# A prologue by feature tiles: the modulation of each tile is made while the dense products run, and x is asked for in halves

## The chip, the cores and the metric

One core of a Trainium2 chip runs the whole program. The metric is device time in microseconds of one execution; smaller is better. The core's engines run beside each other and wait for one another by semaphores: TensorE (PE, with its weight loads PEld), VectorE (DVE), ScalarE (ACT), GpSimd (POOL) and SyncE (SP), which here asks for nearly all transfers.

## The reference, cut to what matters

The reference is a two-block model over 1024 tokens of 1024 features, with 256 context tokens beside them. The change concerns only what comes before the first block's mixer:

```python
def rms_norm(x, g):
    return x * lax.rsqrt(jnp.mean(x * x, axis=-1, keepdims=True) + RMS_EPS) * g

def modulate(h, shift, scale):
    return h * (1 + scale) + shift

mod = jax.nn.silu(c) @ ada_w[l] + ada_b[l]
sh1, sc1, g1, sh2, sc2, g2 = ...          # split in six
csh1, csc1, ... = silu(c_ctx) @ ada_w[l] + ada_b[l]
hc = modulate(rms_norm(ctx, norm1_g[l]), csh1, csc1)
hx = modulate(rms_norm(x, norm1_g[l]), sh1, sc1)
# then both go through w_in, in products of 128 columns at a time
```

So before the first dense product the kernel needs the root of each token's mean square, and for each feature a gain `(1 + scale) * norm1_g` and a shift. Scale and shift for x and context are the first 2048 columns of a product of two vectors of 1024 (silu of c and of c_ctx) with an 8 MB matrix.

## The kernel before

Features lie on partitions: x is held as 8 feature tiles (kt or k, 0 to 7) of 128 partitions by tokens. Tokens are in three groups g: 0 is the context (256 tokens), 1 and 2 are the halves of x (512 each). Each dense product is made with three matmuls per feature tile (high by high, high by low, low by high part), since h and the weights are both split in a high part in a reduced type (h_hi, `fp32r`) and a low part that holds the rest (h_lo). "w", "g", "v", "k", "r" are names of 128-column tiles of w_in; a "chunk" is one such tile for one group of tokens, in one of four PSUM banks.

All of it is in `projections`. Each engine has its own program, in an order written out by hand, and no engine passes an instruction that waits.

SP (lines 251 to 275) asks for: the vectors, matrix tile 0, the context, two sets of constants, matrix tile 1, half 1 of x, matrix tile 2, half 2 of x, matrix tile 3, the weight "w", matrix tiles 4 to 7, c_in, then weights "g", "v", "k". The matrix tiles are cut by input feature: tile i is rows 128i to 128i + 127 with all 2048 output columns, and there are three places for them. All weights pass through one buffer `raw_in`; `load_w` waits until the weight before was split.

TensorE: `modulations` (334 to 351) multiplies the 8 matrix tiles as they land; the sum over tiles is whole only after the last. Between them it makes the sums of squares of the groups (`sums`, L331). Then four small matmuls (L350), the picks, turn the rows of the result into columns, one value per partition. Then `first_dense` (353 to 369) makes "w" of the context and "w" and "g" of both halves together, feature tile by feature tile as the parts of h come. Then `dense("v", 0, 0)` (L105) and all that follows.

ACT: squares and roots of the groups (L615, L619, L621; each root takes two table loads), split of "w" (L530, high part), copy of the modulation rows (L633), then all h_hi (L608), 8 of the context and 16 of x. After them it applies silu to c_row, splits "v" and reads the first chunks.

DVE: folds the squares (L910, L912), multiplies x by the root in three passes (L917), makes the gains (L922, L926), then per feature tile the full value (L936) and h_lo (L941). POOL makes the low parts of the weights (L744).

Rows of the profile name memory by the program's names: b_tmp, b_xin, b_ada_in, b_wpool, b_ps (PSUM). The lines that matter for the picks are these:

```python
for j in range(4):
    mm = nc.tensor.matmul(ps[3][:, 8 * j:8 * (j + 1)], mod_rows[:, P * j:P * (j + 1)], row_picks, start=True, stop=True)
```

## Time and profile before

| | |
|---|---|
| time, median of 3 runs | 2264.8 us (2264.53 to 2266.89) |
| profiled execution, its span | 2265.7 us |
| TensorE busy | 2050.2 us, 90% |
| VectorE busy | 1500.4 us, 66% |
| ScalarE busy | 892.1 us, 39% |
| GpSimd busy | 773.6 us, 34% |
| mean granted TensorE clock | 0.957 |

The profile is of one execution; its span runs from the first to the last instruction and lies 0.9 us above the median of the timed runs. Busy shares are means over stages with different limits: the stretch that the change touches is the first 82 us, 3.6% of the span, in which TensorE is idle for long stretches. A clock of 1.00 is 2.4 GHz, 0.50 is 1.2 GHz.

### The profile page before, as it was taken

Reading aid. Unit: us, or ns where it says so; the run is one execution under the profiler, and the core shown is the slowest. Engines: PE = TensorE matmul, PEld = TensorE weight load, DVE = VectorE, ACT = ScalarE, POOL = GpSimd, SP = SyncE. Lnnn points to the kernel's source line nnn. Section 1 sums busy time; section 2 is a strip of 40 time slices with the busy share of each in tenths; the row PEclk is TensorE's granted clock in tenths of the full one; section 3 lists DMA queues with packets and bytes.
Section 4 is the critical chain, followed back from the end, with each engine's and each line's share of the span. In section 5 each row is a group of like instructions: output and inputs, shape, how many; then the busy total and the mean of one; then the engine's idle time right before and its main releaser. Section 6 shows DMA issues by size and latency. Waiting matters only on the chain. (4 is left out here: it accounts for less than half of the span.)

```text
span 2265.7 us, 37012 instructions
## 1 busy us (share of the span) xinstructions
PE 2050.2 (90%) x15072; PEld 1594.0 (70%) x15072; DVE 1500.4 (66%) x2052; ACT 892.1 (39%) x1445; POOL 773.6 (34%) x460
## 2 busy tenths in 40 slices
PE   4989999837878898999999979999899999999898
PEld 1767677636767676788877768887677776776566
DVE  5777767679774548788988870454746676546644
ACT  5453443414434637333333331443434354333320
POOL 1144433300030145877777724533321111111111
PEclk7999999958899999999999999999999999999899
DMA  7535444597655422122221274523211111102512
GB/s 308 182 122 174 151 141 130 154 264 197 167 177 143 159 75 75 56 84 84 84 76 73 84 272 139 177 73 122 85 56 56 66 38 47 66 19 84 195 47 84
DMA packets 181335, 271.16 MB, mean 120 GB/s; under 512 B 74280, under 2 KB 122024, under 8 KB 176816
## 3 DMA queue, kind: packets, MB, share of 16 engines
q1 hardware_dynamic: 164816, 250.57, 33.9%
q10 hardware_dynamic: 16352, 18.22, 2.7%
q8 instruction: 121, 1.98, 0.4%
q14 instruction: 46, 0.38, 0.1%
HBM read 200.53 MB, written 68.23 MB: 119 GB/s over the span
## 5 line engine op out<-in xcount | busy, mean ns | idle before, releaser
L105 PE MATMUL b_ps<-h_hi,b_wpool 128*128 128x512 f32 (+1 forms) x896 | 277.4, 387 | 10.8 <-POOL b_wpool L744 10.8
L2995 PE MATMUL g_ps<-g_h_hi,w 128*128 128x512 f32 x784 | 260.0, 403 | 6.0 <-ACT g_q L3192 5.9
L3313 POOL TENSOR_TENSOR w<-raw_down,w 128x1024 fp32r<-128x1024 f32 x38 | 94.5, 2488 | 464.6 <-ACT w L3168 464.6
L2262 DVE SCALAR_TENSOR_TENSOR e_vars<-grid,vec,e_vars 128x1024 f32<-128x1024 f32 x168 | 216.0, 1285 | 7.4 <-ACT e_vars L2009 4.2
L105 PEld LDWEIGHTS b_ps<-h_hi,b_wpool 128*128 128x128 f32 x896 | 167.8, 192 | 56.3 <-POOL b_wpool L744 14.4
L2995 PEld LDWEIGHTS g_ps<-g_h_hi,w 128*128 128x128 f32 x784 | 149.3, 190 | 40.8 <-ACT g_q L3192 6.9
L105 PE MATMUL b_ps<-h_lo,b_wpool 128*128 128x512 f32 (+1 forms) x448 | 170.6, 381 | 0.0
L2995 PE MATMUL g_ps<-g_h_lo,w 128*128 128x512 f32 x392 | 156.1, 398 | 0.0
L2674 POOL TENSOR_TENSOR g_down_lo<-raw_down,g_down_hi 128x1408 fp32r<-128x1408 f32 x26 | 86.7, 3339 | 142.5 <-ACT g_down_hi L2574 142.5
L2513 PE MATMUL g_pb<-g_z_hi,g_down_hi 128*128 128x512 f32 x286 | 114.8, 401 | 14.7 <-DVE g_down_lo L2751 9.8
L744 POOL TENSOR_TENSOR b_wpool<-raw_in,b_wpool 128x1024 fp32r<-128x1024 f32 x26 | 67.9, 2611 | 173.2 <-ACT b_wpool L530 173.2
L2513 PE MATMUL g_pb<-g_z_hi,g_down_lo 128*128 128x512 f32 x286 | 113.1, 396 | 0.0
L2513 PE MATMUL g_pb<-g_z_lo,g_down_hi 128*128 128x512 f32 x286 | 112.7, 394 | 0.0
L1989 ACT ACTIVATE e_main_hi<-e_raw_up 128x512 fp32r<-128x512 f32 x68 | 41.9, 622 | 171.2 <-DMA e_raw_up<-w_ffn 168.9
L2103 POOL TENSOR_TENSOR e_main_lo<-e_raw_up,e_main_hi 128x512 fp32r<-128x512 f32 x68 | 92.6, 1365 | 16.0 <-ACT e_main_hi L1989 16.0
L105 PEld LDWEIGHTS b_ps<-h_lo,b_wpool 128*128 128x128 f32 x448 | 86.0, 192 | 15.7 <-issue 1.0
L3090 PE MATMUL g_ps<-g_h_hi,w 128*128 128x512 f32 x224 | 78.5, 421 | 9.1 <-DVE g_sq L3473 3.3
L2995 PEld LDWEIGHTS g_ps<-g_h_lo,w 128*128 128x128 f32 x392 | 74.5, 190 | 16.2 <-issue 0.5
L3465 DVE COPY g_pt<-g_pb 128x512 f32<-128x512 f32 (+2 forms) x144 | 74.2, 552 | 16.6 <-PE g_pb L3056 15.5
L1473 DVE TENSOR_TENSOR c_lm<-c_ps,con_mixer 128x512 f32<-128x512 f32 x80 | 50.7, 684 | 48.6 <-PE c_ps L1253 48.3
L2311 DVE TENSOR_TENSOR e_z<-e_act_g,combine 128x512 f32<-128x512 f32 x42 | 63.9, 1561 | 21.3 <-ACT e_act_g L2022 21.3
L3222 ACT ACTIVATE g_s<-g_logits,g_mx 128x128 f32<-128x128 f32 (+7 forms) x64 | 49.7, 777 | 69.0 <-DVE g_mx L3446 67.5
(524 smaller groups left out, 5284.4 us busy)
## 6 DMA issues: line engine op xcount, KB each, us to landing
e_raw_up<-w_ffn SPq DMA_DIRECT2D x22, 1024.0 KB, 4.9
raw_down<-w_down SPq DMA_DIRECT2D x32, 704.0 KB, 4.2
c_op<-ops SPq DMA_DIRECT2D x40, 512.0 KB, 5.0
raw_down<-w SPq DMA_DIRECT2D x38, 512.0 KB, 3.7
raw_in<-w SPq DMA_DIRECT2D x26, 512.0 KB, 4.2
mod_stage<-ada_rows ACTq DMA_DIRECT2D x24, 512.0 KB, 3.7
zs<-e_z SPq DMA_DIRECT2D x21, 512.0 KB, 2.6
ops<-b_xin SPq DMA_DIRECT2D x20, 512.0 KB, 4.7
```

The lines of the kernel that those rows point to most:

```text
L105: last = nc.tensor.matmul(out, w[:, k, :], x[:, k, cols], start=(k == 0 and n == 0), stop=(k == nk - 1 and n == 2))
L744: TT(weights(s)[1], raw, weights(s)[0].bitcast(F32), ALU.subtract).then_inc(sem("lo"), 1)
L1473: TT(lm[x][u % 2][:, h], quad(bank[x][h]), bc(t["c_tri"][:, x], 1, PAIRS), ALU.mult).then_inc(S("lm", x), 1)
L2103: TT(w_lo[slot], a_of[slot] if i < PLAIN else source[slot], w_hi[slot].bitcast(F32), ALU.subtract).then_inc(sem(f"w_lo{slot}"), 1)
L2262: STT(out=acc, in0=view, scalar=wt, in1=acc, op0=ALU.mult, op1=ALU.add).then_inc(sem("conv"), 1)
L2311: a = TT(z[:, cols(g)], act_g[:, cols(g)], val_of(g, i), ALU.mult)
L2513: mm = nc.tensor.matmul(bank_of(g, j), w[s][:, k], y[:, f], start=(f == 0 and i == 0), stop=(f == NFF - 1 and i == 2))
L2674: nc.gpsimd.tensor_tensor(w_lo[w_slot(n)], raw[:, n % 2], w_hi[w_slot(n)].bitcast(F32), ALU.subtract).then_inc(sem(f"w_lo{n % 2}"), 1)
L2995: mm = nc.tensor.matmul(out_bank, ww[w % 2][:, k], xx[g][:, k], start=(k == 0 and a == 0), stop=(k == KD - 1 and a == 2))
L3090: mm = nc.tensor.matmul(ps[1][:], ww[w % 2][:, k], xx[g][:, k], start=(a == 0 and b == 0), stop=(a == 1 + LAST and b == 2))
L3313: nc.gpsimd.tensor_tensor(w_lo[w % 2], raw[:, w % 2], w_hi[w % 2].bitcast(F32), ALU.subtract).then_inc(sem("lo"), 1)
L3465: nc.vector.tensor_copy(pt[:, h, at // P:to // P].rearrange("p b c -> p (b c)"), turned[u % 2][:, 0:to - at]).then_inc(sem("unturned"), 1)
```

## The change

The modulation matrix is cut by output instead of by input: tile k holds, for all 1024 input features, the 128 shift and 128 scale columns of feature tile k (`"ada"` on the host is transposed to that). So one tile gives the whole shift and gain of one feature tile, and h of that tile can be made before the next tile is multiplied.

TensorE: `modulated(k)` multiplies tile k (8 matmuls of 256 columns, in four column groups), ACT copies the rows (`rows_kept`), `picked(k)` turns them into columns (8 matmuls with 2 moving columns), and ACT makes shift and gain (`gains`). Tiles 0 and 1 come before the dense products, tiles 2 to 7 between them. The order of dense work is a list of pieces, (group, tile): (1,0) (1,1) (2,0) (1,2) (2,1) ... (1,7) (2,6) (2,7), then the context's eight. Only "w" is made by pieces; "g" of both halves is made in one go between the pieces of x and those of the context.

DVE: `input_pre` multiplies x by gain and root in one operation, ACT adds the shift and rounds (`input_high`), DVE makes the low part with the shift added once more (`input_low`). The three passes by the root are gone, and so are the gains on DVE. A product of bias and norm (`gain_of_bias`) is made once at the start.

SP asks for half 1 of x first, in two transfers, then constants, matrix tile 0, weight "w", matrix tile 1, half 2 of x in two transfers, the context, tiles 2 and 3, weight "g", tiles 4 to 7, c_in, the other constants, "v" and "k". The tiles lie in eight places, of which several are other buffers that are free at that time; so tiles 2 and 3 wait for the sums of half 1, 4 and 7 for those of half 2. The first two loads of the second modulation (`load_mod`) come later on ACT, near the end of the pieces.

```diff
-    GADA = KD
     ROOT_SHIFT = 10
-    SLOTS_ADA = 3
-    K_DVE = K_ORDER = tuple(range(KD))
+    PIECES = [(1, 0), (1, 1), (2, 0)] + [(g, k - (g - 1)) for k in range(2, KD) for g in (1, 2)] + [(2, KD - 1)]
+    PIECES += [(0, k) for k in range(KD)]
+    NPIECES = len(PIECES)
+    piece = {x: i + 1 for i, x in enumerate(PIECES)}
...
-    CHUNKS = [("w", 0, 0), ("w", 0, 1), ("g", 0, 1), ("w", 0, 2), ("g", 0, 2)] + [(x, 0, g) for x, g in V0_FIRST]
+    FIRST = [("w", 0, 1), ("w", 0, 2), ("g", 0, 1), ("g", 0, 2), ("w", 0, 0)]
+    CHUNKS = FIRST + [(x, 0, g) for x, g in V0_FIRST]
...
+        rowps = [ps[4 + i][:, 0:2 * P] for i in range(2)]
+        mod_rows = [t["h_spare"][:, 1, KD - 1, CTX + BANK + 2 * P * i:CTX + BANK + 2 * P * (i + 1)] for i in range(2)]
+        mod_cols = [ps[6 + i][:, 0:4].rearrange("p (s c) -> p s c", c=2) for i in range(2)]
...
+        ada_place = [staged, ada_in[:, 1], flat_tmp[:, 0:NADA], flat_tmp[:, NADA:2 * NADA], flat_tmp[:, 2 * NADA:3 * NADA],
+                     staged, ada_in[:, 1], flat_tmp[:, 3 * NADA:4 * NADA]]
+        ada_cols = [place.rearrange("p (i z) -> p i z", z=2 * P) for place in ada_place]
...
+            def load_ada(k):
+                if k in (2, 3):
+                    sp.wait_ge(sem("sumsq"), 1)
+                elif k in (4, 7):
+                    sp.wait_ge(sem("sumsq"), 2)
+                elif k in (5, 6):
+                    sp.wait_ge(sem("ada_used"), k - 4)
+                sp.dma_start(ada_place[k], d["ada"][k]).then_inc(sem(f"ada_in{k}"), 16)
+            def load_x(g):
+                for part in range(2):
+                    rows = slice(4 * part, 4 * part + 4)
+                    sp.dma_start(xin[:, rows, cols(g)], d["xT"][:, rows, seq(g)]).then_inc(sem(f"x{g}{part}"), 16)
+            load_x(1)
+            sp.dma_start(con, d["consts"][:, 0:NKEPT]).then_inc(sem("consts"), 16)
             load_ada(0)
+            load_w(("w", 0))
+            load_ada(1)
+            load_x(2)
             sp.dma_start(xin[:, :, 0:CTX], d["ctxT"]).then_inc(sem("x0"), 16)
-            sp.dma_start(con, d["consts"][:, 0:NKEPT]).then_inc(sem("consts"), 16)
-            sp.dma_start(t["con_mixer"], d["consts"][:, NKEPT:NCON]).then_inc(sem("consts"), 16)
-            for g in (1, 2):
-                load_ada(g)
-                sp.dma_start(xin[:, :, cols(g)], d["xT"][:, :, seq(g)]).then_inc(sem(f"x{g}"), 16)
-            load_ada(3)
-            load_w(("w", 0))
-            for i in range(4, GADA):
-                load_ada(i)
+            for kt in range(2, 4):
+                load_ada(kt)
+            load_w(("g", 0))
+            for kt in range(4, KD):
+                load_ada(kt)
             sp.dma_start(c_row, d["c_in"].broadcast_to([P, D])).then_inc(sem("c_in"), 16)
-            for x in "gvk":
+            sp.dma_start(t["con_mixer"], d["consts"][:, NKEPT:NCON]).then_inc(sem("con_mixer"), 16)
+            for x in "vk":
                 load_w((x, 0))
-            sp.wait_ge(sem("h_lo"), 3 * len(K_DVE))
+            sp.wait_ge(sem("h_lo"), NPIECES)
             load_lora(0)
             sp.wait_ge(sem("read_a"), act_read[("g", 0, 2)])
...
+            def sums(n, g):
+                pe.wait_ge(sem("folded"), 2 * n + 2)
+                if n == 0:
+                    pe.wait_ge(sem("consts"), 16)
+                elif g == 0:
+                    pe.wait_ge(sem("log"), 1)
                 for kt in range(2):
-                    mm = nc.tensor.matmul(ps[g][:, 0:width(g)], t["c_ones"], tmp[:, kt, cols(g)], start=kt == 0, stop=kt == 1)
+                    mm = nc.tensor.matmul(sums_ps[g][:, 0:width(g)], t["c_ones"], squared[g][:, kt], start=kt == 0, stop=kt == 1)
                 mm.then_inc(sem("sumsq"), 1)
...
+            def modulated(k):
+                if k == 0:
+                    pe.wait_ge(sem("silu_c"), 1)
+                    pe.wait_ge(sem("rows_clear"), 2)
+                elif k >= 2:
+                    pe.wait_ge(sem("mod_rows"), k - 1)
+                pe.wait_ge(sem(f"ada_in{k}"), 16)
+                for half in range(2):
                     for b in range(4):
-                        mm = nc.tensor.matmul(rowps[32 * b:32 * b + 2], silu_c[:, i, :], ada_in[:, i % SLOTS_ADA, BANK * b:BANK * (b + 1)],
-                                              start=(i == 0), stop=(i == KD - 1))
-                    mm.then_inc(sem(f"ada_used{i % SLOTS_ADA}"), 1)
-                    if i in SUMS_AFTER:
-                        if i == SUMS_AFTER[0]:
-                            pe.wait_ge(sem("consts"), 32)
-                        sums(SUMS_AFTER.index(i))
-                pe.wait_ge(sem("mod_rows"), 1)
-                for j in range(4):
-                    mm = nc.tensor.matmul(ps[3][:, 8 * j:8 * (j + 1)], mod_rows[:, P * j:P * (j + 1)], row_picks, start=True, stop=True)
+                        i = 4 * half + b
+                        mm = nc.tensor.matmul(rowps[k % 2][32 * b:32 * b + 2], silu_c[:, i, :], ada_cols[k][:, i], start=half == 0,
+                                              stop=half == 1)
+                mm.then_inc(sem("ada_used"), 1)
+            def picked(k):
+                pe.wait_ge(sem("mod_rows"), k + 1)
+                if k >= 2:
+                    pe.wait_ge(sem("gain"), k - 1)
+                for x in range(2):
+                    for b in range(4):
+                        mm = nc.tensor.matmul(mod_cols[k % 2][:, x], mod_rows[k % 2][:, P * x:P * (x + 1)], t["c_ident"][:, 32 * b:32 * b + 2],
+                                              start=b == 0, stop=b == 3)
                 mm.then_inc(sem("mod_cols"), 1)
-            def first_dense(names, g):
-                for x in names:
-                    pe.wait_ge(sem("lo"), tile_no[(x, 0)] + 1)
-                    i = chunk[(x, 0, g)]
+            def first_dense(g, k):
+                pe.wait_ge(sem("h_lo"), piece[(g, k)])
+                i = chunk[("w", 0, g)]
+                if k == 0:
+                    pe.wait_ge(sem("lo"), tile_no[("w", 0)] + 1)
                     if i >= 4:
                         pe.wait_ge(sem("read_a"), act_read[CHUNKS[i - 4]])
-                for k in K_ORDER:
-                    pe.wait_ge(sem("h_lo"), KD * g + k + 1)
-                    for x in names:
-                        w_hi, w_lo = weights(slot[(x, 0)])
-                        out = ps[chunk[(x, 0, g)] % 4][:, 0:width(g)]
-                        for n, (w, h) in enumerate(((w_hi, h_hi), (w_hi, h_lo), (w_lo, h_hi))):
-                            mm = nc.tensor.matmul(out, w[:, k, :], h[:, k, cols(g)], start=(k == K_ORDER[0] and n == 0),
-                                                  stop=(k == K_ORDER[-1] and n == 2))
-                        if k == K_ORDER[-1]:
-                            mm.then_inc(sem("chunk"), 1)
+                w_hi, w_lo = weights(slot[("w", 0)])
+                out = ps[i % 4][:, 0:width(g)]
+                for n, (w, h) in enumerate(((w_hi, h_hi), (w_hi, h_lo), (w_lo, h_hi))):
+                    mm = nc.tensor.matmul(out, w[:, k, :], h[:, k, cols(g)], start=(k == 0 and n == 0), stop=(k == KD - 1 and n == 2))
+                if k == KD - 1:
+                    mm.then_inc(sem("chunk"), 1)
...
-            modulations()
-            first_dense("w", 0)
-            for g in (1, 2):
-                first_dense("wg", g)
+            sums(0, 1)
+            modulated(0)
+            sums(1, 2)
+            picked(0)
+            modulated(1)
+            sums(2, 0)
+            picked(1)
+            for g, kt in PIECES:
+                ahead = kt + 2 if g == 1 and kt + 2 < KD else None
+                if ahead:
+                    modulated(ahead)
+                if (g, kt) == (0, 0):
+                    for x in (1, 2):
+                        dense("g", 0, x)
+                first_dense(g, kt)
+                if ahead:
+                    picked(ahead)
...
+            def rows_kept(k):
+                act.wait_ge(sem("ada_used"), k + 1)
+                if k >= 2:
+                    act.wait_ge(sem("mod_cols"), k - 1)
+                A(mod_rows[k % 2], rowps[k % 2], ACT.Copy).then_inc(sem("mod_rows"), 1)
+            def gains(k):
+                act.wait_ge(sem("mod_cols"), k + 1)
+                if k == 0:
+                    act.wait_ge(sem("gain_of_bias"), 1)
+                A(t["mod"][:, :, k], mod_cols[k % 2][:, 0], ACT.Identity, bias=t["v_ada_b"][:, k:k + 1])
+                A(gain[:, :, k], mod_cols[k % 2][:, 1], ACT.Identity, scale=t["v_norm1_g"][:, k:k + 1],
+                  bias=gain_of_bias[:, k:k + 1]).then_inc(sem("gain"), 1)
+            def input_high(g, k):
+                act.wait_ge(sem("pre"), piece[(g, k)])
                 c = 1 if g == 0 else 0
-                for kt in range(KD):
-                    A(h_hi[:, kt, cols(g)], tmp[:, kt, cols(g)], ACT.Identity, scale=gain[:, c, kt:kt + 1],
-                      bias=t["mod"][:, c, kt:kt + 1]).then_inc(sem("h_hi"), 1)
+                A(h_hi[:, k, cols(g)], xin[:, k, cols(g)], ACT.Identity, bias=t["mod"][:, c, k:k + 1]).then_inc(sem("h_hi"), 1)
+            def squares(g, part):
+                rows = slice(4 * part, 4 * part + 4) if g else slice(0, KD)
+                act.wait_ge(sem(f"x{g}{part}" if g else "x0"), 16)
+                A(squared[g][:, rows], xin[:, rows, cols(g)], ACT.Square).then_inc(sem("squares"), 1)
...
-            squares(0)
-            squares(1)
+            for g in (1, 2):
+                for part in range(2):
+                    squares(g, part)
             act.wait_ge(sem("eps"), 2)
-            roots(0)
-            squares(2)
-            roots(1)
-            roots(2)
+            root_log(0, 1)
+            root(0, 1)
+            squares(0, 0)
+            rows_kept(0)
             hi("w", 0)
-            last = GADA - 1
-            act.wait_ge(sem(f"ada_used{last % SLOTS_ADA}"), last // SLOTS_ADA + 1)
-            A(mod_rows, rowps[:], ACT.Copy).then_inc(sem("mod_rows"), 1)
-            for i in range(2):
-                load_mod(i)
-            inputs_hi(0)
-            hi("g", 0)
-            inputs_hi(1)
-            inputs_hi(2)
+            gains(0)
+            root_log(1, 2)
+            rows_kept(1)
+            root_log(2, 0)
+            root(1, 2)
+            gains(1)
+            root(2, 0)
+            for n, (g, kt) in enumerate(PIECES):
+                input_high(g, kt)
+                if g == 1 and kt + 2 < KD:
+                    rows_kept(kt + 2)
+                if n and PIECES[n - 1][0] == 1 and PIECES[n - 1][1] + 2 < KD:
+                    gains(PIECES[n - 1][1] + 2)
+                if (g, kt) == (1, 3):
+                    hi("g", 0)
+                if (g, kt) == (2, 6):
+                    for i in range(2):
+                        load_mod(i)
...
+            def input_pre(g, k):
                 c = 1 if g == 0 else 0
-                for kt in range(KD + 1):
-                    if kt < KD:
-                        TS(xin[:, kt, cols(g)], tmp[:, kt, cols(g)], gain[:, c, kt:kt + 1], t["mod"][:, c, kt:kt + 1], ALU.mult,
-                           ALU.add).then_inc(sem("full"), 1)
-                    if kt - 1 in K_DVE:
-                        dve.wait_ge(sem("h_hi"), KD * g + kt)
-                        dve.wait_ge(sem("full"), KD * g + kt)
-                        TT(h_lo[:, kt - 1, cols(g)], xin[:, kt - 1, cols(g)], h_hi[:, kt - 1, cols(g)].bitcast(F32),
-                           ALU.subtract).then_inc(sem("h_lo"), 1)
+                dve.wait_ge(sem("gain"), k + 1)
+                if k == 0:
+                    dve.wait_ge(sem("rstd"), (3, 1, 2)[g])
+                STT(out=xin[:, k, cols(g)], in0=xin[:, k, cols(g)], scalar=gain[:, c, k:k + 1], in1=rstd[:, cols(g)], op0=ALU.mult,
+                    op1=ALU.mult).then_inc(sem("pre"), 1)
+            def input_low(g, k):
+                c = 1 if g == 0 else 0
+                dve.wait_ge(sem("h_hi"), piece[(g, k)])
+                STT(out=h_lo[:, k, cols(g)], in0=xin[:, k, cols(g)], scalar=t["mod"][:, c, k:k + 1], in1=h_hi[:, k, cols(g)].bitcast(F32),
+                    op0=ALU.add, op1=ALU.subtract).then_inc(sem("h_lo"), 1)
...
-            folded(0)
-            folded(1)
-            inputs_normed(0)
-            folded(2)
-            inputs_normed(1)
-            inputs_normed(2)
-            gains()
-            for g in range(3):
-                inputs(g)
+            for i in range(2):
+                nc.vector.memset(ps[4 + i][:], 0.0).then_inc(sem("rows_clear"), 1)
+            dve.wait_ge(sem("vecs"), 16)
+            STT(out=gain_of_bias[:], in0=t["v_ada_b"][:, KD:2 * KD], scalar=1.0, in1=t["v_norm1_g"], op0=ALU.add,
+                op1=ALU.mult).then_inc(sem("gain_of_bias"), 1)
+            folded(0, 1)
+            folded(1, 2)
+            folded(2, 0)
+            input_pre(*PIECES[0])
+            for n in range(NPIECES):
+                if n + 1 < NPIECES:
+                    input_pre(*PIECES[n + 1])
+                input_low(*PIECES[n])
...
-        "ada": a["ada_w"][0][:, 0:2 * D].reshape(KD, P, 2 * D),
+        "ada": a["ada_w"][0][:, 0:2 * D].reshape(KD, P, 2, KD, P).transpose(3, 1, 0, 2, 4).reshape(KD, P, 2 * D),
...
```

## Rows read from the trace of the kernel before

**Rows 1.** Timeline of the inputs: start us, length us, engine, line, operation [idle before <-releaser].

```profile
10.02 1.91 ACT L615 ACTIVATE b_tmp<-b_xin 128x2048 f32<-128x2048 f32 x1 [6.52 <-DMA b_xin<-ctxT]
...
20.00 3.62 ACT L615 ACTIVATE b_tmp<-b_xin 128x4096 f32<-128x4096 f32 x1 [8.07 <-DMA b_xin<-xT]
...
27.55 3.62 ACT L615 ACTIVATE b_tmp<-b_xin 128x4096 f32<-128x4096 f32 x1 [0.42 <-DMA b_xin<-xT]
...
41.61 1.04 PE L341 MATMUL b_ps<-b_ada_in,silu_c 128*2 128x512 f32 x8 [1.18 <-DMA b_ada_in<-ada]
```

**Rows 2.** Transfers of the first 60 us: count, KB each, median us to landing.

```profile
b_ada_in<-ada SPq DMA_DIRECT2D x8, 1024.0 KB, 11.4
b_xin<-xT SPq DMA_DIRECT2D x2, 2048.0 KB, 16.5
```

**Rows 3.** The serial tail: timeline, and L350's instructions (ns min/median/max, first and last start).

```profile
43.26 6.02 POOL L744 TENSOR_TENSOR b_wpool<-raw_in,b_wpool 128x1024 fp32r<-128x1024 f32 x1 [42.81 <-ACT b_wpool L530]
...
L350 PE MATMUL b_ps<-con,h_spare x8: 256/256/277, 43.7 to 44.5; 128*128 128x8 f32 x8
...
50.63 0.55 PE L366 MATMUL b_ps<-h_hi,b_wpool 128*128 128x256 f32 x1 [5.86 <-DVE h_lo L941]
```

**Rows 4.** Timeline of TensorE: the second gap and the first matmul of dense(v).

```profile
58.49 0.47 PE L366 MATMUL b_ps<-h_hi,b_wpool 128*128 128x512 f32 x1 [2.35 <-DVE h_lo L941]
...
81.94 0.28 PE L105 MATMUL b_ps<-h_hi,b_wpool 128*128 128x256 f32 x1
```

**Rows 5.** Windows: length, busy us of each engine (instructions), granted clock, DMA share, GB/s.

```profile
39.40:44.80 5.40, 3.12 (x25) 1.16 (x24) 5.40 (x2) 4.22 (x6) 1.54 (x1) 1.00 0.64 244
...
50.60:56.20 5.60, 5.51 (x24) 5.24 (x24) 5.60 (x14) 5.60 (x10) 1.72 (x1) 0.50 0.22 82
...
60.00:63.30 3.30, 3.30 (x9) 2.57 (x9) 3.30 (x7) 3.30 (x6) 0.00 (x0) 0.53 0.03 11
63.30:81.90 18.60, 18.60 (x83) 15.40 (x83) 17.06 (x34) 9.85 (x14) 3.13 (x1) 1.00 0.38 121
```

**Rows 6.** Durations: timeline of 0 to 110 us, and groups by form (busy us, mean ns).

```profile
22.46 1.89 PE L341 MATMUL b_ps<-b_ada_in,silu_c 128*2 128x512 f32 x8 [3.66 <-DMA b_ada_in<-ada]
...
31.84 3.78 PE L331 MATMUL b_ps<-b_tmp,con 128*128 128x512 f32 x4
...
54.31 11.40 ACT L608 ACTIVATE h_hi<-b_tmp,mod,b_gain 128x512 fp32r<-128x512 f32 x16
...
L530 ACT ACTIVATE b_wpool<-raw_in 128x1024 fp32r<-128x1024 f32 x5 | 5.2, 1049 | 6.8 <-DMA raw_in<-w 6.8
...
L619 ACT ACT_TABLE_LOAD x3 | 3.8, 1283 | 0.1
...
L619 ACT ACTIVATE b_rstd<-b_ps,eps 128x512 f32<-128x512 f32 x2 | 1.4, 687 | 3.2 <-PE b_ps L331 3.2
...
L621 ACT ACTIVATE b_rstd<-b_rstd 128x512 f32<-128x512 f32 x2 | 1.3, 630 | 0.0
...
L549 ACT ACTIVATE b_tmp<-b_ps 128x256 f32<-128x256 f32 x1 | 0.4, 365 | 0.0
...
L612 ACT ACTIVATE silu_c<-vec 128x16 f32<-128x16 f32 x1 | 0.2, 216 | 1.3 <-DMA vec<-vecs 1.3
...
L910 DVE TENSOR_TENSOR b_tmp<-b_tmp 128x2048 f32<-128x2048 f32 x2 | 4.6, 2292 | 11.5 <-ACT b_tmp L615 11.5
```

**Rows 7.** POOL's splits of weights to 90 us, and DVE's timeline in the dense stage.

```profile
L744 POOL TENSOR_TENSOR b_wpool<-raw_in,b_wpool x4: 2515/3059/6023, 43.3 to 83.8; 128x1024 fp32r<-128x1024 f32 x4
...
62.95 0.68 DVE L941 TENSOR_TENSOR h_lo<-b_xin,h_hi 128x512 fp32r<-128x512 f32 x1
63.55 0.54 DVE L936 TENSOR_SCALAR b_xin<-b_tmp,b_gain,mod 128x512 f32<-128x512 f32 x1
```

**Rows 8.** Timeline of TensorE behind the stage: its next two waits.

```profile
92.56 0.44 PE L411 MATMUL b_ps<-con,b_tmp 128*128 128x128 f32 x2 [2.12 <-ACT b_tmp L549]
...
150.26 0.79 PE L105 MATMUL b_ps<-h_hi,b_wpool 128*128 128x512 f32 x1 [7.07 <-POOL b_wpool L744]
```

More of the change, by code:

```diff
@@ L169, in projections @@
         raw = t["raw_in"]
-        with nc.sbuf_tensor("b_ada_in", [P, SLOTS_ADA, NADA], F32) as ada_in:
+        with nc.sbuf_tensor("b_ada_in", [P, 3, NADA], F32) as ada_in:
             pass
@@ new lines, in squares, with root_log, root @@
+            def squares(g, part):
+                rows = slice(4 * part, 4 * part + 4) if g else slice(0, KD)
+                act.wait_ge(sem(f"x{g}{part}" if g else "x0"), 16)
+                A(squared[g][:, rows], xin[:, rows, cols(g)], ACT.Square).then_inc(sem("squares"), 1)
+            def root_log(n, g):
+                act.wait_ge(sem("sumsq"), n + 1)
+                A(rstd[:, cols(g)], sums_ps[g][:, 0:width(g)], ACT.Ln, scale=1.0 / D, bias=t["c_eps"]).then_inc(sem("log"), 1)
+            def root(n, g):
+                act.wait_ge(sem("log"), n + 1)
+                A(rstd[:, cols(g)], rstd[:, cols(g)], ACT.Exp, scale=-0.5).then_inc(sem("rstd"), 1)
@@ L643, in _ @@
             mods = 2
-            for x, g in (("w", 0), ("w", 1), ("g", 1), ("w", 2), ("g", 2)):
+            for x, _, g in FIRST:
                 src = there(x, 0, g)
@@ L962, in _ @@
             dve.wait_ge(sem("c_row"), 1)
+            dve.wait_ge(sem("con_mixer"), 16)
             biases(0)
```

74 lines of the change are left out of this document (19 added, 55 removed).

## Prediction, written before the result was known

> **What bounds the kernel now.** I read the timeline of the first 100 us first, since the change touches nothing later, then the prologue's stages by window, then the waits of TensorE behind it. Three stretches show.
> To 41.6 us the DMA queues are full and everything waits for bytes [rows 1]. Only SP's queue carries the inputs, and they land in the order asked for: the squares of the first half of x start at 20.00 us and those of the second at 27.55 us, and between the two landings lie one matrix tile and one half of x, 3072 KB [rows 2]. That is 2.46 us per 1000 KB. The context's squares start at 10.02, behind two transfers of 1024 KB and the vectors.
> From 41.6 to 50.6 us is a serial tail: last matrix tile, copy of the rows (L633), picks (L350), then gains that stand on DVE behind a normalising pass and behind POOL's 6.02 us split of the first weight (43.26 to 49.28); the first dense matmul that waits for h_lo starts at 50.63 [rows 3].
> From 50.6 to 81.94 us TensorE runs the "w" and "g" products: 24 matmuls of 256 columns, a wait of 2.35 us, then 96 of 512 columns. At 81.94 the first matmul of dense("v", 0, 0) starts [rows 4]; I take it as the mark by which both kernels are compared. There TensorE is at the slow level (1.2 GHz) from 50.6 to 56.2 and again from 60.0 to 63.3, and at 2.4 GHz from 63.3 on, 83 matmuls in 18.60 us or 0.224 us each [rows 5]. I use 0.227, since ends are overlapped: 96 x 0.227 = 21.8.
>
> **When the new kernel's TensorE can begin.** The two parts of half 1 of x are two transfers of 1024 KB behind the vectors, as tile 0 and context were, so they land at 7.5 and 10.0; then by 2.46 us per 1000 KB and the shapes in the code: constants (337 KB) 10.8, matrix tile 0 13.4, weight w (512 KB) 14.6, tile 1 17.1, second half of x 19.7 and 22.2, context 24.7, tiles 2 and 3 27.2 and 29.8. So x is whole at 22.2 instead of 27.5.
> ACT takes both halves' squares before its first root. From 22.2: squares of 2048 elements 1.91 -> 24.1; table load, Ln, table load, Exp for half 1 (1.28 + 0.69 + 1.28 + 0.63) -> 28.0; context squares 1.91 -> 29.9; rows_kept(0), taken at 0.36 as a 256-wide copy -> 30.3; split of w 1.04 -> 31.3 [rows 6]. DVE folds half 2 from 24.1: 2.29 and about 1.2 for the half as wide second step -> 27.6; TensorE's sums at the slow level take 3.78 -> 31.4 [rows 6].
> picked(k) appears nowhere in the old trace in this shape. It is 8 float32 matmuls with a 128-column stationary tile and 2 moving columns. The old pick is 4 matmuls with 8 columns: 8 weight loads whose matmuls start from 43.7 to 44.5, 0.8 / 7 = 0.114 apart, at the fast level [rows 3]. So I take 16 x 0.114 = 1.8 us: the loads set the pace, and 2 columns for 8 save nothing. At the slow level all of TensorE's rates halve (1.89 us for a tile against 1.04 at the end [rows 1, 6]), so up to 3.6. The lower bound is zero, were the loads hidden.
> Then in one line of dependence: picked(0), part slow -> 34.1; gains(0), two tiny ACT operations (nearest row: 0.22 for 128x16 [rows 6]) 0.45 -> 34.6; table load and Ln 1.97 -> 36.6; rows_kept(1) -> 37.3 with the wait for modulated(1) and the context sums; picked(1) -> 39.1, while ACT does Ln, load and Exp until 39.7; gains(1) -> 40.1; root of the context 0.42 -> 40.5; first h_hi 0.69 -> 41.2; first h_lo 0.68 -> 41.9. TensorE starts at 42.0: 8.6 us ahead of 50.6. The first weight's low part is ready by 34.4 (31.9, once DVE's context fold is done, + 2.5, POOL's shortest [rows 7]). Of the added waits this one queues most: SP stands before the weight of "g" until then, and tiles 4 to 7 behind it, and who waits for those is TensorE in the pieces. They land at 40 to 48 us, tile 4 being asked for at 48. Both bounds of the split are 2.5 and 6.02; with 6.02 tile 4 lands at 43.5, still early. SP's waits for the sums come free at 19.2 and 31.4, while the queue is full or SP stands anyway; TensorE's own waits for the copied rows lie behind three dense matmuls (0.68) and take ACT 0.36.
>
> **What TensorE now has in that stage.** Before, matrix tiles were multiplied while TensorE waited for bytes, and the picks cost 1.06 us once. Now six of the eight tiles are modulated and picked between the dense matmuls of "w".
> - modulated(k): same columns as before in two halves of 256, four column groups side by side: 1.0 us each at the fast level, 1.89 at the slow [rows 6]. Five behind the start at 42.0: 5.0.
> - picked(k): 6 x 1.8 = 11.0.
> - 16 pieces of 3 matmuls: 48 x 0.227 = 10.9.
> Sum 26.9 -> 68.9. DVE needs pre and low per piece, 0.60 + 0.60 (a row of 0.68 whose successor starts 0.60 later [rows 7]), so 1.2 us, or 2.4 for two pieces; ACT needs 2 x 0.71 + 0.36 + 0.45 = 2.2 [rows 6]; TensorE 2 x 0.68 + 1.0 + 1.8 = 4.2. TensorE is the pace. Only at the end does DVE show: gains(7) can come no earlier than 65.2, DVE stands in order at input_pre(1, 7) until then, and has seven 512-wide operations and one 256-wide one to the last h_lo: 65.2 + 7 x 0.6 + 0.35, and the overlap of the last -> 69.9. The last "w" piece ends at 70.6. Then "g", 48 x 0.227 = 10.9 -> 81.5, and "w" of the context, 24 x 0.12 (half of 0.227, rounded up) = 2.9 -> 84.4. That is 2.5 us behind 81.94, with every stretch at the fast level.
> The old stage paid the slow level about 2.6 + 1.6 us (24 x 0.107 more, and half of 3.3) [rows 5]. The new one starts after an idle 1.9 us and spends 1.8 of every 4.2 us in picks, so I take one such slow stretch, 1.6. Mark: 86.0, 4.1 us late.
> Removed work that is worth nothing: the three normalising passes on DVE and the old gains; they lay beside DMA and, in the tail, are already in the 8.6 us. The moved c_in and con_mixer loads have 20 us of slack. POOL's split of "g" may hold DVE for 2.5 us in the pieces; DVE runs up to three pieces ahead of a pace of 4.2 per pair, which covers it; without that cover it costs 2.5.
> ACT's wait for its 24 pieces puts its first read of "w" behind the last context piece: DVE 69.9 + 8 x 0.67 = 75.3, table load, c_silu and split of "v" (1.28 + 1.05 + 1.05) -> 78.7, read of ("w", 1) 1.2 -> 79.9. TensorE asks for that bank at 81.5. It is a floor, not a wait.
>
> **Behind the mark.** The next stall is at 90.5, where TensorE waits 2.12 us for ACT, which stands at the split of "r" [rows 8]; its weight is asked for after POOL's split of "k", which follows ACT's read of the last "w" product. This chain starts from the mark's own end, so it moves with it. So does the 7.07 us wait at 150.26 [rows 8]: it hangs on DVE and ACT work that starts from norm_sums on TensorE. Nothing fixed in time stands there, so a shift is passed on whole. Modulation loads 2 to 5 start behind ACT's first read (79.9; now they start with the last h_lo), no more than the mark is late.
> Profiled span 2265.7; the three timed runs have their median at 2264.8, 0.9 below, and I subtract that. 2265.7 + 4.1 - 0.9 = 2268.9, rounded to 2269.0. Its own range: 2266 (all fast, picked(0) too) to 2273 (two more slow stretches and POOL uncovered).
>
> **Rivals.**
> Faster: picks cost next to nothing, as loads are taken ahead behind the dense matmuls. Then DVE is the pace: 42.0 + 16 x 1.2 + 0.6 = 61.8, "g" 72.7, and ACT's floor moves with DVE (61.2 + 5.3 + 3.4 + 1.2 = 71.1), "w" of the context 75.6: 6.3 us early, 2258.5. Against it: in the old pick the loads stand 0.114 apart with nothing between; nothing can hide 16 loads behind 2 columns each. It decides below 0.04 us per load. 0.15.
> Much slower: TensorE stays at 1.2 GHz through the pieces. The place is picked(k), the condition that weight loads with 2 moving columns don't hold the level. Each pair then costs 2 x 1.28 + 1.89 + 3.6 = 8.1 instead of 4.2, six pairs 23 us, plus some 2 for a later start: 2264.8 + 2.5 + 25 = 2292 if it lasts, 2273 if a quarter of it does. For it: the level fell at 60.0 after the gap of 2.35 us [rows 4, 5]. Against it: from 39.4 to 44.8 it held with TensorE busy 3.12 of 5.40 us [rows 5]. It decides if the level falls once in the pieces and doesn't come back. 0.20. The Trainium skill, "TensorE: Matmul & The Clock Gate", Part 4: PE-mode transpose, says that transposes don't count as busy in the same way for the clock; the picks are not transposes in name but do one. By that rule the rival holds; no row here shows it for picks.
> No effect: the late mark is swallowed by the 7.07 us wait at 150.26, because the SP and DVE chain there hangs on loads and stores that are not late, 2264.8. Against it, the order just told. 0.15.
> The forecast: 0.50.
>
> **How the numbers follow.** This kernel's measurement tells about 0.2% (4.5 us) from no change: 2260.3 to 2269.3. The forecast's own range is cut by the upper bound: 0.30 within, 0.20 slower. Faster rival 0.15 faster; slow clock 0.20 slower; no effect 0.15 within. So faster 0.15, same 0.45, slower 0.40. The range goes from 2258 (the faster rival) to 2290, which leaves out the clock rival's longest case, about 0.05.
>
> **What would show it.** picked(k) as 16 matmuls in 1.8 us at the fast level; the first dense matmul near 42; TensorE without waits for h_lo between 42 and 65, and waits only in the last five pieces; the pieces' end near 70; dense("v", 0, 0) near 86; the granted clock of 42 to 70 near 1.0. Wrong if: TensorE waits for h_lo from the start (DVE or ACT is the pace), tiles land later than 48, POOL's first split blocks DVE, or the two waits of [rows 8] change length.

## The result, and the profile after

| | before | after |
|---|---|---|
| median, us | 2264.66 (4 runs, 2260.45 to 2266.89) | 2287.38 (4 runs, 2277.66 to 2290.18) |
| ratio, 95% interval | | 1.0089, 1.0065 to 1.0113 |
| span of the profiled execution, us | 2265.7 | 2285.9 |
| granted clock, mean of the span | 0.957 | 0.947 |
| mark (first matmul of dense("v", 0, 0)), us | 81.94 | 101.46 |

The kernel is slower by about 1%: the ratio is 1.0089, and the medians lie 22.7 us apart. The mark is 19.5 us later and the span 20.2 us longer, so the loss is made in the first 100 us.

First the part before TensorE starts on the pieces: timeline of after (start us, length us, engine, line, operation, idle before and its releaser), to be held against [rows 1, 3]. In after's lines picked(k) is L381, modulated(k) L370, sums L356, first_dense L396; on DVE the piece's first operation is L989 and h_lo L996, POOL's splits are L813.

```profile
7.10 1.91 ACT L670 ACTIVATE b_tmp<-b_xin 128x2048 f32<-128x2048 f32 x1 [3.64 <-DMA b_xin<-xT]
9.93 1.91 ACT L670 ACTIVATE b_tmp<-b_xin 128x2048 f32<-128x2048 f32 x1 [0.92 <-DMA b_xin<-xT]
...
22.22 1.91 ACT L670 ACTIVATE b_tmp<-b_xin 128x2048 f32<-128x2048 f32 x1 [0.64 <-DMA b_xin<-xT]
...
31.34 3.41 PE L381 MATMUL b_ps<-con,h_spare 128*128 128x2 f32 x16
34.68 1.89 PE L370 MATMUL b_ps<-b_ada_in,silu_c 128*2 128x256 f32 x16
36.50 2.08 PE L356 MATMUL b_ps<-b_tmp,con 128*128 128x256 f32 x4
38.37 3.41 PE L381 MATMUL b_ps<-con,h_spare 128*128 128x2 f32 x16
41.71 1.89 PE L370 MATMUL b_ps<-b_tmp,silu_c 128*2 128x256 f32 x16
44.08 0.79 PE L396 MATMUL b_ps<-h_hi,b_wpool 128*128 128x512 f32 x1 [0.48 <-DVE h_lo L996]
```

x lands when it was expected to, and the dense matmuls (L396) begin at 44.08 where the old ones began at 50.63. But picked(0) and picked(1) take 3.41 us each: TensorE is at the slow level. Now one pair of pieces, the windows (length, then busy us of PE, PEld, DVE, ACT, POOL with their instructions, granted clock, DMA share, GB/s) and DVE beside POOL:

```profile
44.69 0.63 PE L396 MATMUL b_ps<-h_lo,b_wpool 128*128 128x512 f32 x1
45.09 0.63 PE L396 MATMUL b_ps<-h_hi,b_wpool 128*128 128x512 f32 x1
45.52 3.40 PE L381 MATMUL b_ps<-con,h_spare 128*128 128x2 f32 x16
48.86 1.89 PE L370 MATMUL b_ps<-b_tmp,silu_c 128*2 128x256 f32 x16
...
52.12 3.41 PE L381 MATMUL b_ps<-con,h_spare 128*128 128x2 f32 x16
...
59.99 1.84 PE L381 MATMUL b_ps<-con,h_spare 128*128 128x2 f32 x16
61.69 0.48 PE L396 MATMUL b_ps<-h_hi,b_wpool 128*128 128x512 f32 x1
...
68.03 0.79 PE L396 MATMUL b_ps<-h_hi,b_wpool 128*128 128x512 f32 x1 [1.56 <-DVE h_lo L996]
```

```profile
34.00:58.00 24.00, 23.52 (x125) 16.82 (x129) 7.03 (x10) 10.05 (x21) 0.06 (x1) 0.50 0.62 246
58.00:66.00 8.00, 7.79 (x63) 5.55 (x55) 3.31 (x6) 4.04 (x8) 0.92 (x1) 0.89 0.00 0
66.00:70.00 4.00, 2.44 (x15) 1.33 (x17) 3.96 (x4) 1.11 (x3) 1.43 (x1) 0.57 0.39 109
70.00:84.00 14.00, 12.65 (x82) 8.67 (x74) 7.47 (x11) 6.01 (x13) 0.00 (x0) 0.74 0.02 8
...
40.00:80.00 40.00, 37.54 (x234) 26.49 (x233) 17.79 (x23) 14.57 (x35) 2.34 (x1) 0.67 0.30 116
```

```profile
65.08 2.34 POOL L813 TENSOR_TENSOR b_wpool<-raw_in,b_wpool 128x1024 fp32r<-128x1024 f32 x1 [31.03 <-ACT b_wpool L571]
...
65.65 2.32 DVE L996 SCALAR_TENSOR_TENSOR h_lo<-b_xin,mod,h_hi 128x512 fp32r<-128x512 f32 x1 [1.22 <-ACT h_hi L665]
67.90 0.74 DVE L989 SCALAR_TENSOR_TENSOR b_xin<-b_xin,b_gain,b_rstd 128x512 f32<-128x512 f32 x1
68.56 0.74 DVE L996 SCALAR_TENSOR_TENSOR h_lo<-b_xin,mod,h_hi 128x512 fp32r<-128x512 f32 x1
```

The clock is 0.50 from 34 to 58 us although PE is busy 23.52 of 24.00 us: the engine isn't short of work, it does it at half the rate. The fast level comes back just before 60, at the end of the longest run of other matmuls so far (no picks from 55.4 to 60.0), and a set of picks then takes 1.84 us. At 68.03, behind a wait of 1.56 us, the level is gone again; it returns at 73.4, falls once more at 80.2, with a wait of 1.15 us, and is back at 87.0. Of the 43.6 us from 44.08 to 87.71 some 29 are slow. The wait of 1.56 us is DVE's: an h_lo that takes 0.75 us elsewhere takes 2.32 and ends 0.55 us behind POOL's split of "g". The last piece of x starts its final matmul at 87.48; "g" takes 87.71 to 98.59 (10.9 us) and "w" of the context 2.9, both as in the sum.

Behind the mark the two waits of [rows 8] are these:

```profile
113.56 0.44 PE L440 MATMUL b_ps<-con,b_tmp 128*128 128x128 f32 x2 [3.59 <-ACT b_tmp L590]
...
171.20 0.79 PE L105 MATMUL b_ps<-h_hi,b_wpool 128*128 128x512 f32 x1 [7.08 <-POOL b_wpool L813]
```

The second has moved by 20.9 us and kept its length (7.07 before); the first is 1.5 us longer.

### The profile page after: what moved, and what is told of

Same layout as the page of the kernel before. It is cut to its first block and busy times, and to the rows that moved or that the text cites. A ratio compares the mean times of both kernels' runs of the same rounds, so it can differ in the third digit from the quotient of the medians.

```text
span 2285.9 us, 37389 instructions
## 1 busy us (share of the span) xinstructions
PE 2081.9 (91%) x15256; PEld 1623.4 (71%) x15256; DVE 1495.6 (65%) x2047; ACT 895.1 (39%) x1468; POOL 768.1 (34%) x460
## 5 line engine op out<-in xcount | busy, mean ns | idle before, releaser
L105 PE MATMUL b_ps<-h_hi,b_wpool 128*128 128x512 f32 (+1 forms) x928 | 287.9, 388 | 10.7 <-POOL b_wpool L813 10.7
L105 PEld LDWEIGHTS b_ps<-h_hi,b_wpool 128*128 128x128 f32 x928 | 174.1, 192 | 57.2 <-POOL b_wpool L813 14.3
L105 PE MATMUL b_ps<-h_lo,b_wpool 128*128 128x512 f32 (+1 forms) x464 | 176.6, 381 | 0.0
L813 POOL TENSOR_TENSOR b_wpool<-raw_in,b_wpool 128x1024 fp32r<-128x1024 f32 x26 | 64.1, 2467 | 198.0 <-ACT b_wpool L571 198.0
```

Source lines behind the costliest of these rows:

```text
L105: last = nc.tensor.matmul(out, w[:, k, :], x[:, k, cols], start=(k == 0 and n == 0), stop=(k == nk - 1 and n == 2))
L813: TT(weights(s)[1], raw, weights(s)[0].bitcast(F32), ALU.subtract).then_inc(sem("lo"), 1)
```

## The experiments

All times are medians, each set beside runs of the kernel before on the same chip, whose own median was 2264.8 to 2269.3; ratios are to those, estimated from the single runs, and so not exactly the quotients of the medians. One measure is used throughout: the mark, of the profiled execution.

**Do the picks hold the clock down?** The same 16 weight loads, in the same order behind the same waits, with 128 moving columns for 2 (the reads of mod_cols, left out here, still take the first two):

```diff
-mod_cols = [ps[6 + i][:, 0:4].rearrange("p (s c) -> p s c", c=2) for i in range(2)]
+mod_cols = [ps[6 + i][:, 0:2 * P].rearrange("p (s c) -> p s c", c=P) for i in range(2)]
-mm = nc.tensor.matmul(mod_cols[k % 2][:, x], ..., t["c_ident"][:, 32 * b:32 * b + 2], ...)
+mm = nc.tensor.matmul(mod_cols[k % 2][:, x], ..., con[:, 32 * b:32 * b + P], ...)
```

> The changed kernel, but each pick moves 128 columns past its weights instead of 2 (the 126 others are not used). Weight loads, their number and all waits stay as they are; at either clock level a pick is paced by its weight load (0.114 us fast, 0.213 us slow), and 128 float32 columns take about as long, so the picks' own time should not grow. Theory (picks with 2 moving columns count as a pause of TensorE, so the clock falls): TensorE is at the fast level through most of 48 to 80 us, picks take 1.8 us each, dense("v", 0, 0) starts near 86 instead of 101.5, and the time is 4 to 8 us above the kernel before on the same chip instead of 20. Rival A (it is the 2-column stationary tile of modulated, or small matmuls as such, or waits for DVE): the slow level stays, mark near 101, 20 us above. Rival B (128 columns cost time of their own): picks over 2.5 us even at the fast level, more than 25 us above.

Beside it, on the same chip, the changed kernel as it is:

> The changed kernel itself, beside the others on the same chip, to compare levels run by run: 13 to 25 us above the kernel before, the spread being the clock: mark between 92 and 102 us, everything behind the mark the same.

d_wide_pick: 2271.96 us (10 runs), ratio 1.0029 (1.0011 to 1.0047), mark 90.00. d_after_again: 2288.39 us (4 runs), ratio 1.0101 (1.0076 to 1.0126), mark 101.62. Two windows and the picks of d_wide_pick:

```profile
34.00:58.00 24.00, 20.84 (x187) 15.01 (x186) 11.24 (x15) 14.04 (x31) 2.47 (x2) 1.00 0.62 246
...
40.00:80.00 40.00, 33.83 (x252) 24.01 (x242) 28.11 (x44) 19.80 (x44) 2.35 (x1) 1.00 0.39 147
```

```profile
42.62 1.95 PE L381 MATMUL b_ps<-con,h_spare 128*128 128x128 f32 x16
...
46.27 1.95 PE L381 MATMUL b_ps<-con,h_spare 128*128 128x128 f32 x16
47.97 0.47 PE L396 MATMUL b_ps<-h_hi,b_wpool 128*128 128x512 f32 x1
...
59.05 0.50 PE L396 MATMUL b_ps<-h_hi,b_wpool 128*128 128x512 f32 x1 [1.36 <-DVE h_lo L996]
...
70.40 0.50 PE L396 MATMUL b_ps<-h_hi,b_wpool 128*128 128x512 f32 x1 [1.29 <-DVE h_lo L996]
71.73 0.50 PE L396 MATMUL b_ps<-h_hi,b_wpool 128*128 128x512 f32 x1 [0.36 <-DVE h_lo L996]
```

and the window of d_after_again:

```profile
40.00:80.00 40.00, 37.54 (x233) 26.50 (x234) 17.80 (x23) 14.50 (x35) 2.35 (x1) 0.67 0.30 116
```

This decides it. With 64 times the moving columns the record of a set of picks is 0.1 us longer than with 2 at the fast level (1.95 against 1.84), the next matmul starts 1.70 us behind the first pick in both, and at the slow level the narrow set takes 3.41. The granted clock is 1.00 in every window from 34 to 100 us, and 16.4 us of the 23.6 are back, 11.6 of them at the mark (101.62 to 90.00). So the slow level that goes with the picks of 2 columns is the largest part of the loss at the mark, 11.6 of 19.7 us. (The other 4.8 us of the 16.4 arise behind the mark, and no run shows why; see the end of the next section.) The mark is 4 us later than expected, and rivals A and B are both out. It isn't that they transpose, for the wide ones do the same transposition. Nor does busy time tell the two apart: PE is busy less in the faster kernel, 33.83 us against 37.54.

What is left, 7.2 us in the time and 8.1 us at the mark, has the picks' own time and the waits for DVE in it; the next kernels take these apart.

**What if there are fewer loads?** The four picks of a half differ only in the block of the identity; as they add up in one bank, one matmul with the summed blocks does the same. 4 instructions instead of 16, still with 2 columns:

```diff
-for b in range(4):
-    mm = nc.tensor.matmul(..., t["c_ident"][:, 32 * b:32 * b + 2], start=b == 0, stop=b == 3)
+mm = nc.tensor.matmul(..., pick_sum[:, 0:2], start=True, stop=True)
```

> The changed kernel, but the four picks per half are one matmul with a moving matrix that already sums the four row groups: 2 matmuls of 2 moving columns per tile instead of 8, the same result. Theory (the picks are the added cost, and the slow level doubles it): a pick takes 0.46 us fast or 0.85 slow. TensorE starts near 40, two pieces with a tile cost it 2.8 us fast, DVE at 0.67 per operation is then as slow, pieces end near 62, mark near 76 to 80, time 2259 to 2263. If the slow level stays all the same: two pieces 2.56 + 1.89 + 0.85 = 5.3 us, mark near 91, 2274. Rival (the picks are not what costs, DVE or the order is): mark stays above 95, time above 2280.

2277.39 us (10 runs), ratio 1.0031 (1.0020 to 1.0043), mark 87.47.

```profile
39.77 0.50 PE L398 MATMUL b_ps<-h_hi,b_wpool 128*128 128x512 f32 x1 [2.94 <-DVE h_lo L998]
...
44.32 0.50 PE L383 MATMUL b_ps<-b_pick_sum,h_spare 128*128 128x2 f32 x4
45.43 0.50 PE L398 MATMUL b_ps<-h_hi,b_wpool 128*128 128x512 f32 x1 [0.61 <-DVE h_lo L998]
...
55.62 0.79 PE L398 MATMUL b_ps<-h_hi,b_wpool 128*128 128x512 f32 x1 [3.19 <-DVE h_lo L998]
```

```profile
55.00:64.00 9.00, 8.38 (x45) 4.33 (x45) 5.39 (x8) 2.11 (x5) 0.02 (x1) 0.50 0.21 59
```

A set costs 0.50 us. Now TensorE waits for DVE in nearly each pair, 3.19 us at POOL's split of "g", and behind that wait the level is 0.50 for 9 us. It also falls for some 3 us shortly behind the wait of 2.94 us ahead of the first piece. Work taken off TensorE turns into waits first, and the level falls at the two longest of them. The expectation, which counted no such waits, had the mark at 76 to 80, or at 91 with the slow level throughout.

Both at once, summed blocks and 128 columns:

> The changed kernel with 2 picks per tile instead of 8, and each moves 128 columns. With 8 wide picks the level stayed at 2.4 GHz and the mark came at 89.6; with 2 narrow ones it fell after a wait of 3.19 us for DVE. Theory: two pieces with a tile cost TensorE 2.8 us, DVE 2.66 (0.665 between its starts), so DVE is the pace from about 40: 16 pieces x 1.33 = 21.3, plus POOL's split of "g" (2.5) -> 64.5, "g" 10.9, context 2.9 -> mark near 78.5, 3 us before that of the kernel before: 0 to 5 us faster than it on the same chip. If TensorE waits enough for DVE to lose the level (as with narrow summed picks), mark 82 to 88 and 1 to 8 us slower.

> The kernel with summed, wide picks once more, for a second trace: its first trace was of its fastest run (2269.7), the other seven were 2272 to 2282. Theory (TensorE loses the level in the pieces in most runs): this trace has the slow level for 5 to 15 us more between 40 and 70, and a mark of 85 to 90. Rival: mark near 82.3 again, the difference lies behind it.

d_sum_wide: 2276.61 us (8 runs), ratio 1.0046 (1.0031 to 1.0062); sum_wide_look is one more run of it, on another chip. Two profiled executions of the same kernel differ: mark 83.80 (span 2267.8) and 87.20 (span 2273.0, time 2275.01). In the second the level was 0.50 from 40 to 46:

```profile
40.00:46.00 6.00, 5.75 (x27) 3.53 (x28) 2.08 (x4) 1.66 (x5) 0.00 (x0) 0.50 1.02 431
```

The first profile was the fastest of its eight runs, so the second is likely the more typical; the level is lost at the first wait of 2.71 us in the second and not in the first. With 4 picks per set these traces don't tell 2 columns from 128: the mark with 2, 87.47, is no later than the later of these by more than 0.3 us. Both show the split of "g" and the wait that it makes. Here the first:

```profile
51.00 2.34 POOL L815 TENSOR_TENSOR b_wpool<-raw_in,b_wpool 128x1024 fp32r<-128x1024 f32 x1 [16.92 <-ACT b_wpool L573]
```

```profile
51.57 2.33 DVE L998 SCALAR_TENSOR_TENSOR h_lo<-b_xin,mod,h_hi 128x512 fp32r<-128x512 f32 x1 [1.93 <-ACT h_hi L667]
```

```profile
53.95 0.50 PE L398 MATMUL b_ps<-h_hi,b_wpool 128*128 128x512 f32 x1 [3.08 <-DVE h_lo L998]
```

**Fill the waits with "g"?** "g" by pieces, four behind "w", and its split after piece (1, 1):

```diff
 for n, (g, kt) in enumerate(PIECES):
     ...
+    if 4 <= n < NX:
+        gate_dense(*PIECES[n - 4])
...
-                if (g, kt) == (1, 3):
+                if (g, kt) == (1, 1):
                     hi("g", 0)
```

> As the one with summed, wide picks, and "g" of each half is multiplied by pieces too, four pieces behind "w", instead of in one go after them; the split of "g" comes after piece (1, 1) instead of (1, 3). Theory: TensorE has 4.2 us of work for two pieces with a tile, 2.7 for two without, against DVE's 2.66, so it hardly waits: the level stays high, and after the last piece only 4 x 0.68 = 2.7 us of "g" are left instead of 10.9. But the context pieces wait for ACT's first read of "w" (the floor of the prediction, 5.9 us of context pieces on DVE, then 3.4 + 1.2 on ACT), so the mark comes at about 64.5 + 5.9 + 4.6 + 2.9 = 78, no earlier than with "g" in one go. If that floor is wrong, mark near 71.

2277.14 us (9 runs), ratio 1.0047 (1.0025 to 1.0070), mark 87.94: no gain over d_sum_wide, whose mark was 83.80 and 87.20. TensorE doesn't wait for h_lo any more between 48.31 and the end of "g"; waits of 2.71 and 3.48 us ahead of that stay, and a new one follows:

```profile
83.13 0.55 PE L398 MATMUL b_ps<-h_hi,b_wpool 128*128 128x256 f32 x1 [5.36 <-ACT b_tmp L732]
```

TensorE is through with both products of x at 83.13 - 5.36 = 77.8, 3.2 us ahead of d_sum_wide (83.80 less 2.9 for the context), and then waits for the bank that ACT reads only behind its last context piece. That is the floor of the prediction, 79.9 there, in the open. Behind it the level is slow, and the context's products take 4.8 us instead of 2.9. Next, ACT reads "w" of both halves between its context pieces:

```diff
+    if g == 0 and kt in (3, 6):
+        w_read(1 if kt == 3 else 2)
```

> As the one before, and ACT reads "w" of both halves between the context pieces (after tiles 3 and 6) instead of after c_silu and the split of "v". Theory (ACT's read is the floor): the context pieces are then paced by DVE only, mark near 73 to 75, 6 to 9 us faster than the kernel before on the same chip. Rival (dense("v", 0, 0) then waits for the split of "v", which ACT makes last): mark near 78 with the wait moved to "v", nothing gained over the one before.

2283.73 us (4 runs), ratio 1.0076 (1.0058 to 1.0094), mark 87.47. The wait has moved one step on and is nearly as long:

```profile
87.47 0.58 PE L105 MATMUL b_ps<-h_hi,b_wpool 128*128 128x256 f32 x1 [4.83 <-POOL b_wpool L835]
```

This time dense("v") waits for its split weight, which ACT and POOL make after the pieces. So a second resource stood right behind the first, and a TensorE ahead of the pieces' pace can't use its lead.

**Move the split out of the pieces.** From the kernel with summed, wide picks (d_sum_wide): ACT splits "w" between the squares of the two halves, SP asks for "g" ahead of tiles 2 and 3, and its split comes ahead of gains(0):

```diff
+                if g == 1:
+                    hi("w", 0)
...
-            hi("w", 0)
+            hi("g", 0)
...
-                if (g, kt) == (1, 3):
-                    hi("g", 0)
```

> As the one with summed, wide picks, and the splits of the first two weights are moved to where DVE has nothing to do: "w" is split by ACT between the squares of the two halves of x, so SP asks for "g" before tiles 2 and 3, and "g" is split where "w" was, before the first gains. Theory: the 3.1 us wait for h_lo at 54 in the trace of that kernel is POOL's split of "g" in DVE's way; it goes, DVE is the pace from 39 at 1.33 us per piece, pieces end near 61, mark 75 to 78 instead of 82.3, time 3 to 7 us below the kernel before if the level stays, and level with it if TensorE loses the level in the pieces, since it is then 1.28 + 1.28 + 1.89 + 0.85 = 5.3 us for two pieces. Rival (the median of the one before, 11.6 us above the kernel before with a mark only 2.3 us late, comes from something behind the mark): the time stays 8 us or more above what the mark says.

2270.84 us (10 runs), ratio 1.0012 (0.9992 to 1.0032), mark 82.21. The wait of 3.1 us is gone; the one of 2.71 ahead of the first piece stays, behind which the level falls once more (0.72 from 40 to 46), and so do 0.56 per pair and 0.36 per piece. The mark was expected at 75 to 78 and the time 3 to 7 us below before's, or level with it if the clock fell; it is 4.2 us above, which is within the noise. The waits that stay, and the level:

```profile
53.48 0.51 PE L398 MATMUL b_ps<-h_hi,b_wpool 128*128 128x512 f32 x1 [0.56 <-DVE h_lo L998]
...
65.26 0.50 PE L398 MATMUL b_ps<-h_hi,b_wpool 128*128 128x512 f32 x1 [0.36 <-DVE h_lo L998]
```

```profile
34.00:40.00 6.00, 3.06 (x29) 1.75 (x26) 2.50 (x4) 5.77 (x12) 0.16 (x1) 1.00 1.00 423
40.00:46.00 6.00, 5.23 (x31) 3.08 (x31) 2.70 (x5) 2.31 (x7) 0.00 (x0) 0.72 1.00 377
46.00:69.00 23.00, 19.11 (x125) 10.91 (x125) 18.83 (x30) 12.73 (x28) 0.00 (x0) 1.00 0.22 80
```

Last, the waits are filled with matmuls whose output nobody reads (eight ahead of the first piece, one ahead of each of the last five of x):

```diff
+                if (g, kt) == (1, 0):
+                    fill(8)
+                elif g and (g, kt) in PIECES[11:]:
+                    fill(1)
```

> As the one before, with idle work for TensorE where it waits for h_lo: 8 float32 matmuls of 128 columns before the first piece (1.8 us at the fast level) and one before each of the last five of x, into a corner of PSUM that nobody reads. Theory (a wait for DVE loses the level, and the loss differs from run to run): the granted clock is 1.0 from 34 to 75 us in the trace, runs spread less, and the median is 2 to 5 us below the one without. Rival (the level is not lost there): no difference, or 2 us worse when the filling runs at the slow level.

2272.32 us (10 runs), ratio 1.0017 (0.9995 to 1.0040), mark 80.61, the only one ahead of before's 81.94. The level is 1.00 throughout:

```profile
34.00:67.00 33.00, 27.95 (x203) 18.14 (x202) 23.36 (x36) 20.24 (x45) 0.00 (x0) 1.00 0.51 197
```

The mark's 1.3 us don't show in the time, and neither do the 2 to 5 us that were expected of a level that holds: the median is 1.5 us above early_split's, and the runs spread no less (2260.28 to 2280.18). With the picks, the split and the waits repaired, the new order is level with the old one within the noise; none of these kernels is shown to beat it.

## Where the prediction was right and which step of it failed

The main forecast (2269.0, with 2266 to 2273 as its own range) failed, and the rival that it gave a chance of 0.20 held: 2287.38 lies between that rival's 2273 and 2292. It lies in the stated range of 2258 to 2290 too, but only because the range takes in most of that rival; that is no merit of the forecast's mechanism. By step:

- **Landings and the way to the first piece: right.** Squares of x at 7.10, 9.93 and 22.22, expected 7.5, 10.0 and 22.2. Sums end and picked(0) starts at 31.34, expected 31.4. First dense matmul expected at 42.0: 44.08 in after, 41.82 in d_wide_pick. So the 2.3 us between these two are the slow level ahead of the first piece, in the picks and in the modulation and sums beside them, and "plus some 2 for a later start" of the rival was right.
- **The level in the pieces: the step that failed.** "I take one such slow stretch, 1.6", and against the rival stood that the level had held with TensorE busy 3.12 of 5.40 us [rows 5]. That argument went by busy time, and busy time doesn't tell the cases apart: 23.52 of 24.00 us at 0.50 in after, 20.84 of 24.00 at 1.00 in d_wide_pick. In the old window TensorE ran modulation matmuls with 512 moving columns beside its 8 picks [rows 1, 3]; the new picks keep it busier, and the level stays at 0.50 through them. The rival's price per pair, 8.1 us, was about right: from the picks at 52.12 to those at 59.99, with two pieces and one modulation, are 7.9 us. It lasted for two thirds of the stage (29 of 43.6 us), with returns at 59.7, 73.4 and 87.0.
- **picked(k) = 16 x 0.114 = 1.8 us: right.** 1.84 at the fast level, 3.41 at the slow (3.6 said). The columns don't set it: with 64 times as many the next matmul starts 1.70 us behind the first pick as before. (The sum has 11.0 for six sets; 6 x 1.8 is 10.8.) The rule of the Trainium skill ("TensorE: Matmul & The Clock Gate", Part 4: PE-mode transpose), that transposes don't count as busy in the same way, is stated for matmuls with the transpose mode on. The picks are plain matmuls; the rule pointed to the right rival, but d_wide_pick shows that transposing isn't the reason here: its picks do the same transposition and the level holds.
- **DVE's 0.60 per operation: too small.** The new operations have two tensor inputs and a scalar each (L989, L996): 0.74 to 0.75 us, successors 0.67 apart, so 1.33 us per piece for 1.2. The old row that I took [rows 7] was of another form, with no scalar. At TensorE's 4.2 us per pair it is hidden; in the last pieces it shows as 0.36 us per piece, as DVE's 1.33 stands against 0.97 of TensorE (three matmuls and the wait's own start).
- **POOL's split of "g", "covered": wrong.** "DVE runs up to three pieces ahead" fails because gains(k) comes out of TensorE's own picks, so DVE waits for ACT and TensorE and never builds the lead: in after it is idle 1.2 to 3.0 us before seven of the ten h_lo between 52 and 81 us. The cost without cover was put at 2.5; it is 1.56 in after, 1.36 in d_wide_pick, and 3.1 once the picks are short.
- **All fast, the mark at 84.4: too early.** d_wide_pick has the fast level throughout, and its mark is 90.00, 5.6 later. It takes 34.4 us from the first piece to the end of the last (41.82 to 76.24) where the sum of TensorE's work had 26.9. Waits for h_lo are 4.7 of that (0.33, 0.31, 1.36, 0.32, 1.29 and three of 0.36 or 0.37). The 16 pieces take 14.0 us instead of 10.9, 0.80 and more each for 0.68: the 0.227 per matmul comes from the old, unbroken row of dense matmuls, and the first matmul behind other work takes 0.31 to 0.34 until the next starts. The picks take 0.4 less than the 11.0, the modulation 0.1 more. Of these 7.5 us the forecast had 1.7 (the DVE tail), and the stage began 0.2 early; 5.6 are left. So even at the fast level the change was worth about 5.6 us less than its sum. That the "own range" of 2266 to 2273 holds d_wide_pick's 2271.96 is partly luck: its mark is 8.1 us late and its span only 4.2 longer.
- **"g" 10.9 and context 2.9: right** (10.9 and 2.9). **The shift is passed on whole: it came out so for the change.** Mark +19.5, the 7.07 us wait +20.9 with its length kept, span +20.2; the rival "no effect" is excluded. In d_wide_pick and early_fill the shift wasn't kept, as the next paragraph tells. The 2.12 us wait didn't keep its length (3.59).

**What stays open.** Behind the mark the kernels don't keep their distances to some 5 us: d_wide_pick's mark is 8.1 us late and its span 4.2 longer, early_fill's is 1.3 early and its span 5.3 longer. The stage from about 465 to 740 us, with the same code in all kernels, took, from the first to the last of one line's matmuls, 267.2 us in before, 262.7 in after, 262.5 in d_wide_pick and 273.7 in early_fill. Sixteen executions of before itself on one chip lie between 2255.06 and 2276.85. Single traces can't say whether the prologue has a part in that, so differences of some 4 us behind the mark aren't attributed.

## What to carry to other kernels

Before small matmuls are put between large ones, ask what they do to TensorE's level, not only how long they take: here columns that nobody needs, at 0.1 us per set or less, brought the mark 11.6 us forward. Before a lead is counted, follow the loop: when work is interleaved so that one engine's input comes out of the other's output in the same loop, count no lead for either; a split on POOL then shows in full. And when a lead is won, look for the second resource right behind the first: ACT's read of a bank and then the split of "v" took back all that "g" by pieces had won.
